# A dense feed-forward in three high/low fp32r passes, with seven ring slots for the dense stages

## What is computed

```python
def swiglu(h, w_gate, w_up, w_down):
    return (jax.nn.silu(h @ w_gate) * (h @ w_up)) @ w_down

hn = rmsnorm(h, norm_ffn[0])
h = h + swiglu(hn, ffn_w_gate[0], ffn_w_up[0], ffn_w_down[0])   # 1024 -> 3584 -> 1024
```

## Time and profile before

| | |
|---|---|
| median of 3 executions | 1668.14 us |
| the profiled execution | 1667.81 us, of which its span is 1666.0 us |
| TensorE, matmuls | 1572.7 us busy (94% of the span) |
| TensorE, weight loads | 1383.5 us (83%) |
| VectorE | 1033.7 us (62%) |
| ScalarE | 813.3 us (49%) |
| DMA | 425.16 MB, mean 255 GB/s |

### The profile page before, as it was taken

The page is one execution under the profiler, slowest core; times in us unless marked ns, Lnnn a source line. Parts: engine busy times, 40 slices in busy tenths (PEclk is TensorE's granted clock), DMA queues, the critical chain, the costliest instruction groups (busy, mean ns, idle before and its releaser), DMA issues.

```text
span 1666.0 us, 23792 instructions
## 1 busy us (share of the span) xinstructions
PE 1572.7 (94%) x9865; PEld 1383.5 (83%) x9865; DVE 1033.7 (62%) x1120; ACT 813.3 (49%) x865; POOL 0.2 (0%) x4
## 2 busy tenths in 40 slices
PE   5998999999877879999999999999999999999995
PEld 4887888888655669998998988899898898898893
DVE  5531000000144348988888888888888888888883
ACT  2511000000123227767676766767667767767662
POOL 0000000000000000000000000000000000000000
PEclk8999999999987879999999999999999999999997
DMA  9043444448211218999999999999999999999920
GB/s 347 31 149 104 152 152 151 154 153 327 99 51 51 73 55 332 357 345 352 356 342 352 357 342 350 358 344 347 358 343 347 361 347 344 363 341 344 367 83 26
DMA packets 62050, 425.16 MB, mean 255 GB/s; under 512 B 7805, under 2 KB 10106, under 8 KB 10746
## 3 DMA queue, kind: packets, MB, share of 16 engines
q1 hardware_dynamic: 60240, 422.60, 68.4%
q10 hardware_dynamic: 1706, 1.06, 0.2%
HBM read 422.59 MB, written 1.05 MB: 254 GB/s over the span
## 4 chain that ended last, share of the span: by engine, by line
PE 90%; DVE 4%; ACT 3%; issue 2%; ACTq 0%; DMA 0%; DVEq 0%
PE ps L1282 35%; PE ps L1004 21%; PE ps L1304 19%; PE ps L1086 6%; PE ps L1252 2%; PE ps L1270 2%; PE ps L1289 1%; DVE w_lo L886 1%; ACT w_hi L534 1%; PE ps L995 1%; DVE hn L698 1%; DVE scratch L772 1%; PE ps L1126 0%; DVE xg_mem L696 0%; PE ps L1215 0%
## 5 line engine op out<-in xcount | busy, mean ns | idle before, releaser
L886 DVE TENSOR_TENSOR w_lo<-ring,w_hi 128x2048 fp32r<-128x2048 f32 x336 | 766.4, 2290 | 126.1 <-ACT w_hi L534 120.3
L534 ACT CAST w_hi<-ring 128x2048 fp32r<-128x2048 f32 x336 | 640.0, 1910 | 263.5 <-PE ps L1282 212.1
L1004 PE MATMUL ps<-hn,ring 128*128 128x256 f32 x1312 | 304.1, 394 | 17.7 <-issue 9.0
L1004 PEld LDWEIGHTS ps<-hn,ring 128*128 128x128 f32 x1312 | 260.3, 199 | 59.3 <-issue 16.7
L1282 PE MATMUL ps<-w_hi,xg_hi 128*96 128x256 f32 x1792 | 246.6, 280 | 2.5 <-ACT w_hi L534 2.5
L1282 PE MATMUL ps<-w_lo,xg_hi 128*96 128x256 f32 x1792 | 242.2, 277 | 1.6 <-DVE w_lo L886 1.6
L1282 PE MATMUL ps<-w_hi,xg_lo 128*96 128x256 f32 x1792 | 241.7, 277 | 0.0
L1282 PEld LDWEIGHTS ps<-w_hi,xg_hi 128*96 128x96 f32 x1792 | 221.4, 162 | 16.0 <-DVE xg_lo L892 2.6
L1282 PEld LDWEIGHTS ps<-w_lo,xg_hi 128*96 128x96 f32 x1792 | 215.1, 161 | 3.2 <-DVE w_lo L886 3.2
L1282 PEld LDWEIGHTS ps<-w_hi,xg_lo 128*96 128x96 f32 x1792 | 216.0, 162 | 0.0
L743 DVE TENSOR_TENSOR work<-ps,work 128x256 f32<-128x256 f32 x28 | 11.9, 425 | 267.8 <-ACT work L475 267.8
(11 more groups left out here) (220 smaller groups left out, 931.9 us busy)
## 6 DMA issues: line engine op xcount, KB each, us to landing
ring<-in_moe_w_gate SPq DMA_DIRECT2D x112, 1024.0 KB, 5.5
ring<-in_moe_w_up SPq DMA_DIRECT2D x112, 1024.0 KB, 5.8
ring<-in_moe_w_down SPq DMA_DIRECT2D x112, 1024.0 KB, 5.7
ring<-in_ffn_w_gate SPq DMA_DIRECT2D x14, 1024.0 KB, 4.9
ring<-in_ffn_w_up SPq DMA_DIRECT2D x14, 1024.0 KB, 4.9
ring<-in_ffn_w_down SPq DMA_DIRECT2D x14, 1024.0 KB, 4.9
ring<-in_lru_w_in SPq DMA_DIRECT2D x8, 1024.0 KB, 10.2
ring<-in_attn_w_qkv SPq DMA_DIRECT2D x6, 1024.0 KB, 11.7
```

Source lines behind the costliest of these rows:

```text
L534: nc.scalar.copy(w_hi[:, n % PARTS], ring[:, s]).then_inc(hi_done, 1)
L886: V.tensor_tensor(w_lo[:, n % PARTS], ring[:, ORDER_MOE[n % SLOTS]], w_hi[:, n % PARTS].bitcast(F32), ALU.subtract).then_inc(lo_done, 1)
L1004: mm = nc.tensor.matmul(ps[:, bank, c0:c0 + T], w[:, k, col:col + P], rhs[:, k], start=(k == 0), stop=(k == KC - 1))
```

## The change

The dense feed-forward is computed as the experts are. ScalarE casts each of the 42 weight pieces to float32r (`split_ffn`), VectorE makes the low part, hn is split once into `u_hi` and `u_lo` ahead of the products, each chunk's product of silu and up into `f_hi` and `f_lo`, and TensorE makes three passes over each piece, of 16 matmuls each; the weights stay stationary. The loop over two passes of 7 chunks is written out as one sequence of 14. The banks of the down products are opened at the first down piece, and their closing matmuls are gone: the last products close them, and `f_acc` tells of the first three in the last pass.

Since `w_hi` and `w_lo` are now in use from the dense stage on, the scratch of the other stages moves into ring slots 7 to 10, and the split activations overlay slots 11 to 13. All dense stages, the recurrent block and attention load into slots 0 to 6 in turn. The experts' first seven loads use the same seven slots, the others wait for the router's first matmul. The splits of the experts are counted on from the 42 of the dense stage.

```diff
-LRU_LOADS, ATT_LOADS = 13, 10
-ORDER_FFN = [13, 0, 1, 2, 3, 4, 5]
-ORDER_ATT = [6, 7, 8, 9, 10, 11, 12, 13, 0, 1]
-ORDER_MOE = [2, 3, 4, 5] + ORDER_ATT
+LRU_LOADS, FFN_LOADS, ATT_LOADS = 13, PIECES, 10
+FIRST_FFN = LRU_LOADS
+FIRST_ATT = FIRST_FFN + FFN_LOADS
+DENSE_LOADS = FIRST_ATT + ATT_LOADS
+SPLITS = FFN_LOADS
+ORDER_MOE = [(DENSE_LOADS + n) % DENSE for n in range(DENSE)] + list(range(DENSE, SLOTS))
...
-        scr = scratch[:, :]
+        scr = ring[:, DENSE:DENSE + 4, :].rearrange("p s n -> p (s n)")
...
-        slot_of = list(range(LRU_LOADS)) + 6 * ORDER_FFN + ORDER_ATT
+        slot_of = [k % DENSE for k in range(DENSE_LOADS)]
...
+            def load_dense(k, kind, w, c0):
+                s, last = slot_of[k], k - DENSE
+                if FIRST_FFN <= last < FIRST_ATT:
+                    sp.wait_ge(lo_done, last - FIRST_FFN + 1)
+                elif last >= FIRST_ATT:
+                    sp.wait_ge(used, last - FFN_LOADS + 1)
+                elif last >= 0:
+                    sp.wait_ge(used, last + 1)
...
-                    sp.wait_ge(lo_done, PIECES * i + (n + 1))
-                    if n < SLOTS:
-
-                        sp.wait_ge(used, FIRST_MOE - SLOTS + 1 + n)
+                    if first and n < SLOTS:
+                        sp.wait_ge(used, LRU_LOADS + min(ATT_LOADS, ATT_LOADS - DENSE + n + 1))
+                    else:
+                        sp.wait_ge(lo_done, PIECES * i + (SPLITS - SLOTS + n + 1))
...
+            def split_ffn(j):
+
+                act.wait_ge(loaded[slot_of[FIRST_FFN + j]], arrive[FIRST_FFN + j])
+                if j >= PARTS:
+                    act.wait_ge(parts_used, j - PARTS + 1)
+                nc.scalar.copy(w_hi[:, j % PARTS], ring[:, slot_of[FIRST_FFN + j]]).then_inc(hi_done, 1)
+
+            for j in range(PARTS):
+                split_ffn(j)
             squares(1)
             root(1, 7)
-
-
-            for t in range(2):
-                for c in range(HALF):
+            for c in range(KC):
+                act.wait_ge(hn_ready, KC + c + 1)
+                nc.scalar.copy(u_hi[:, c], hn[:, c]).then_inc(u_hi_ready, 1)
+
+
+            for j in range(PARTS, FFN_LOADS + 1):
+                if j < FFN_LOADS:
+                    split_ffn(j)
+                what, c = FFN_PIECES[j - PARTS] if j < FFN_LOADS else ("up", NCH - 1)
+                if what == "up":
                     for f in range(2):
-                        act.wait_ge(f_gu, 2 * HALF * t + (2 * c + f + 1))
+                        act.wait_ge(parts_used, FFN_AT["up", c] + 1)
                         nc.scalar.activation(ffn_h[:, c % 2, f], ps[:, 2 * (c % 2) + f, 0:T], ACT.Silu).then_inc(f_silu, 1)
+                    for f in range(2):
+                        act.wait_ge(f_h, 2 * c + f + 1)
+                        nc.scalar.copy(f_hi[:, c % 2, f], ffn_h[:, c % 2, f]).then_inc(f_hi_ready, 1)
...
+            for j in range(PARTS):
+                split_ffn(j)
             for c in range(KC):
                 dve.wait_ge(o_proj, c + 1)
                 V.tensor_tensor(h[:, c], ps[:, c % 4, 0:T], h[:, c], ALU.add).then_inc(h_ready, 1)
             dve.wait_ge(h_ready, 2 * KC)
             normed(1, "ffn0")
-
-            for t in range(2):
-                for c in range(HALF):
+            for c in range(KC):
+                dve.wait_ge(u_hi_ready, c + 1)
+                V.tensor_tensor(u_lo[:, c], hn[:, c], u_hi[:, c].bitcast(F32), ALU.subtract).then_inc(u_ready, 1)
...
+            def ffn_gate_up(what, c):
+                j, m = FFN_AT[what, c], int(what == "up")
+                w = [a.rearrange("p (k c) -> p k c", k=KC) for a in ffn_parts(j)]
+                us = (u_hi, u_lo)
+                for a, b in PASSES:
+                    if b:
+                        pe.wait_ge(lo_done, j + 1)
                     for f in range(2):
-                        pe.wait_ge(f_h, 2 * HALF * t + (2 * c + f + 1))
-                        for d in range(KC):
-                            mm = nc.tensor.matmul(ps[:, 4 + d // 2, (d % 2) * T:(d % 2 + 1) * T], as_rows(s)[:, f, d * P:(d + 1) * P],
-                                                  ffn_h[:, c % 2, f], start=False, stop=False, skip_group_check=True)
-                            if f == 0 and d == 0 and c < HALF - 1:
+                        for k in range(KC):
+                            if j == 0 and f == 0 and b == 0:
+                                pe.wait_ge(u_ready if a else u_hi_ready, k + 1)
+                            mm = nc.tensor.matmul(ps[:, 2 * (c % 2) + f, m * T:(m + 1) * T], w[b][:, k, f * P:(f + 1) * P], us[a][:, k],
+                                                  start=(k == 0 and (a, b) == (0, 0)), stop=(k == KC - 1 and b == 1))
+                            if j == 0 and (a, b, f, k) == (0, 0, 0, 0):
                                 mm.then_inc(used, 1)
-                    mm.then_inc(used, 1)
...
+            for what, c in FFN_PIECES:
+                if what == "down":
+                    if c == 0:
+                        pe.wait_ge(rms_ready, 2)
+                        pe.wait_ge(zero_ready, 1)
+                        for b in range(4, 8):
+                            nc.tensor.matmul(ps[:, b, :], zero[:, 0:P], zero[:, :], start=True, stop=True)
+                    ffn_down(c)
+                else:
+                    if what == "gate" and c >= 2:
+                        pe.wait_ge(f_h, 2 * c - 2)
+                    ffn_gate_up(what, c)
```

More of the change, by code:

```diff
@@ L131, in sem @@
             return ctx.enter_context(nc.semaphore(name))
+        with (nc.sbuf_tensor("below", [P, 11 * SLOT], F32), nc.sbuf_tensor("u_hi", [P, KC, T], F32R) as u_hi,
+              nc.sbuf_tensor("u_lo", [P, KC, T], F32R) as u_lo, nc.sbuf_tensor("f_hi", [P, 2, 2, T], F32R) as f_hi,
+              nc.sbuf_tensor("f_lo", [P, 2, 2, T], F32R) as f_lo):
+            pass
         ring = sb("ring", [P, SLOTS, SLOT])
@@ L296, in pieces @@
             return seq
-        FFN_PIECES = pieces(HALF, 1)
+        FFN_PIECES = pieces(NCH, 1)
         FFN_AT = {piece: j for j, piece in enumerate(FFN_PIECES)}
@@ L337, in _ @@
             for k, (kind, w, c0) in enumerate(early):
[L338 to L352, removed]
+                load_dense(k, kind, w, c0)
+            ffn_w = {"gate": ffn_w_gate[0], "up": ffn_w_up[0], "down": ffn_w_down[0]}
+            for j, (what, c) in enumerate(FFN_PIECES):
+                load_dense(FIRST_FFN + j, "r" if what == "down" else "c", ffn_w[what], c if what == "down" else CHF * c)
             late = [(w_qkv, D), (w_qkv, D + CHF)] + [(w_qkv, CHF * t) for t in range(4)]
@@ L378, in _ @@
             NEXT_BODY = [(what, c, 1) for what, c, _ in BODY]
-            load(0, 0, 0, LEAD + BODY)
+            load(0, 0, 0, LEAD + BODY, first=True)
             with sp.Fori(0, E - 1) as i:
@@ L635, in _ @@
                 V.memset(xpad[:, b, 0:3], 0.0).then_inc(zero_ready, 1)
-            V.memset(small[:, 160:161], 0.0).then_inc(lo_done, SLOTS)
             V.memset(small[:, 96:160], 0.0).then_inc(zero_ready, 1)
@@ L731, in _, with split_ffn @@
                 V.tensor_tensor(yy[:, t], rr[:, t], yy[:, t], ALU.mult).then_inc(z_ready, 1)
+            def split_ffn(j):
+                dve.wait_ge(hi_done, j + 1)
+                V.tensor_tensor(w_lo[:, j % PARTS], ring[:, slot_of[FIRST_FFN + j]], w_hi[:, j % PARTS].bitcast(F32),
+                                ALU.subtract).then_inc(lo_done, 1)
+            for j in range(PARTS):
+                split_ffn(j)
             for c in range(KC):
@@ L883, in split @@
             def split(i, n):
-                dve.wait_ge(hi_done, PIECES * i + (n + 1))
-                V.tensor_tensor(w_lo[:, n % PARTS], ring[:, ORDER_MOE[n % SLOTS]], w_hi[:, n % PARTS].bitcast(F32),
+                part = (SPLITS + n) % PARTS
+                dve.wait_ge(hi_done, PIECES * i + (SPLITS + n + 1))
+                V.tensor_tensor(w_lo[:, part], ring[:, ORDER_MOE[n % SLOTS]], w_hi[:, part].bitcast(F32),
                                 ALU.subtract).then_inc(lo_done, 1)
@@ L1105, in _, with ffn_parts @@
-            for b in range(4, 8):
-                nc.tensor.matmul(ps[:, b, :], zero[:, 0:P], zero[:, :], start=False, stop=True, skip_group_check=True).then_inc(f_acc, 1)
+            PASSES = ((0, 0), (1, 0), (0, 1))
+            def ffn_parts(j):
+                pe.wait_ge(hi_done, j + 1)
+                return w_hi[:, j % PARTS], w_lo[:, j % PARTS]
+            def ffn_gate_up(what, c):
[5 more added lines that the diff above has]
+                        pe.wait_ge(lo_done, j + 1)
+                    for f in range(2):
+                        for k in range(KC):
[4 more added lines that the diff above has]
+                            if j == 0 and (a, b, f, k) == (0, 0, 0, 0):
+                                mm.then_inc(used, 1)
+                mm.then_inc(parts_used, 1)
@@ new lines, in ffn_down @@
+            def ffn_down(c):
+                j = FFN_AT["down", c]
```

(15 more changed lines are left out.)

91 lines of the change are left out of this document (34 added, 57 removed).

## The result

The changed kernel takes 1616.4 us (median of four executions, 1613.92 to 1620.1), the kernel before 1668.25 us beside it: a ratio of 0.9692 with a 95% interval of 0.9671 to 0.9713. It is 3.1% faster. The profiled execution took 1615.43 us, its span is 1613.3 us; the forecast was 1613.0, on the profiled execution of before.

A forecast was written before the change was run, and what follows sets the result against it. TensorE's unbroken dense-stage matmuls were taken as the bound. Stage -59.6, end -1.3, wait +4.1 and clock +2.0 summed to -54.8 us, from 1667.8 to 1613.0 us; range 1600 to 1634.

The forecast's parts named there:

- Three passes hide their weight loads: Dense stage: 128-column weight loads overlap the 256-element streams in all 2016 fp32r matmuls, as the experts' 96-column loads do.
- first rival: Dense stage: 128-column loads don't quite hide, 119 to 130 ns a matmul, kernel at 1623 to 1645 us; chance 12%.
- the second (225 ns): Rival for the dense stage: weight load fully exposed, 225 ns a matmul, kernel at 1836 us; chance 4%.
- 114.3 ns a matmul: Dense stage: pace taken from the experts' passes, giving 5.49 us a piece and 230.4 us for 42 pieces.
- First piece +1.6: Dense stage's start: waiting for casts, half clock and low parts makes the first piece 1.6 us longer than a steady one.
- opening +0.9: Dense stage: four bank-opening matmuls ahead of the first down piece, no longer inside a wait, add 0.9 us.
- end -1.3: Dense stage's end: closing matmuls go and additions into h start in the last pass, saving 1.3 us.
- The added wait, +4.1: After o_proj: weight splits ahead of residual additions delay the first sum of squares, TensorE idles, 4.1 us added.
- Half clock behind that wait, +2.0: After TensorE's idle behind o_proj: a stretch at half clock costs 0 to 3.4 us, taken as 2.0.
- ScalarE and VectorE hidden: Dense stage: per chunk ScalarE's 7.3 us and VectorE's 8.6 us fit beside TensorE's 16.5 us.
- Loads hidden: Dense and experts' stages: weight loads arrive before they are needed, experts' late ones by over 10 us; cost nil.
- Attention keeps its time: Attention stage: its work and time stay unchanged, except half-clock stretches falling otherwise, one worth up to 3.4 us.

The follow-up runs named there:

- e3: The changed kernel with dense-stage matmuls loading 96 weight columns instead of 128, a quarter of the output rows left out: 1613.36 us (one execution).
- e2: The changed kernel with the first three weight splits put between the residual additions and squares instead of ahead of them: 1612.37 us, ratio 0.9666.
- e11: The changed kernel with five 512-wide bf16 matmuls of zeros ahead of the last down piece: 1611.44 us, ratio 0.9661.
- e1: The changed kernel with the four bank-opening matmuls put back ahead of the first gate piece: 1609.61 us, ratio 0.9646.
- e4: The changed kernel with only the first of three passes in the dense stage, low parts still made: 1484.3 us (one execution).
- e7: e1 with one further 512-wide bf16 matmul of zeros ahead of the down piece of chunk 7: 1600.4 us, ratio 0.9601.
- e9: The changed kernel with the splits interleaved as in e2 and no bank-opening matmuls, first down products starting the accumulation: 1595.35 us, ratio 0.9565.
- e10: e9 with the experts' f32 scatter and gather matmuls ahead of the down piece instead of behind it: 1593.25 us, ratio 0.9591.
- e12: e9 with eight 512-wide bf16 matmuls of zeros ahead of the last down piece: 1611.4 us, ratio 0.9673.
- e8: e9 with four 512-wide fp32r matmuls, result unused, after the first gate piece: 1603.96 us, ratio 0.9616.

## Why the prediction was right, and where its terms were off

The time fell in the range, 3.4 us over the forecast, and the mechanism was the one forecast. That it is as near as this is in part luck: the pace cost 6.4 us more than forecast, and two terms that depend on the execution gave 3.6 back. Step by step:

- **Three passes hide their weight loads.** Right. 2016 single records, unbroken, and e3 prices the 32 more columns at 1.1 ns. The first rival (119 ns or more) and the second (225 ns) did not come. The rule on row groups, which the Trainium skill states in "TensorE: Matmul & The Clock Gate", Part 3, taken by itself, is contradicted by this trace too: a load of 128 columns, 128 rows high, goes unseen beside a stream of 256 at 113.3 ns. I read it too narrowly: the same Part, under "The mechanism", also lets a load go ahead of running matmuls where it targets the background weight buffer. With that the trace would agree; no run here shows which buffer a load goes to.
- **114.3 ns a matmul.** The term that was mis-sized. I took the mean of 113.5 ns (256 wide) and 115.8 (512 wide) from one pair of stretches, and left the other stretches' 117 ns to the bounds and the first rival, as if it were noise. They are two modes. The stage had some 160 matmuls at 113.3 and 1820 at 117.8: +6.4 us. 2016 times 1.0 ns less than my 114.3 and 2016 times 3.5 ns more is -2.0 and +7.1 us: the working should have given about 1611 and 1620 us, with a chance for each.
- **First piece +1.6, opening +0.9, end -1.3.** Measured 1.5 (144.96 less 137.96 less 5.49), 0.96 and -1.4.
- **The added wait, +4.1.** Right in place, cause and size: 3.8 us, ended by VectorE's addition, and in e2 gone but for 0.7.
- **Half clock behind that wait, +2.0.** It did not come in this execution; the tiles behind the gap take 3.45 us each. In e11's profile, after a gap of 3.71 us, one tile took 5.14: 1.7 us, beside 3.4 us at the half clock; e3's has 3.4 us of it at the same place. The gap is 3.5 to 3.6 us in e1, e4 and e7, where it did not come. So the bound was right and the value a matter of the execution.
- **ScalarE and VectorE hidden.** Right; e4 shows at what pace they would not be.
- **Loads hidden.** Right: the only wait for a dense load is that of the third cast, inside the added wait; the late loads of the experts cost nothing (1064.0 us in both, from the router's first matmul to the end).
- **Attention keeps its time.** Right for this kernel and by luck: 161.2 and 160.9. I had allowed one half-clock stretch, 3.4 us. e7, e9 and e10 show that the same stage can take 153, so the allowance was too small by half.

The misses, +6.4 for the pace, -2.0 for the clock, -1.6 for the earlier o_proj and -0.7 in the small ones, leave 2.1 us between the forecast -54.8 and the measured -52.7.

## What to carry to other kernels

Where rows of one and the same instruction form show two paces, don't average them: ask which one the new stream will be in, and forecast both. A matmul stream should not be broken by odd instructions that can stand elsewhere or go: four of 0.96 us in all came with a slower pace for 1820 others here, and without them (e9) all five executions kept to one group. And work that an engine does ahead of time belongs between the small operations that others wait for, not in front of them.

## What the runs showed of the hardware that I had not expected

- An fp32r stream of 256 elements a matmul runs in one of two paces, 113.3 ns or 117.8 ns (128 weight columns; with 96, 116.7 at the slower), both at full granted clock and without idle, with the same work of VectorE and ScalarE beside it. In the dense stage it keeps the pace for as long as like matmuls follow each other. Four to eight bf16 matmuls of zeros were followed by the other pace in four cases (113.3 to 117.8 in the changed kernel, e2 and e12, 117.8 to 113.3 in e11) and by the same in two (the openings of e3 and e11), one alone by the same (e7). What picks the pace at the start stays open: it differs between executions whose instructions are the same so far (e1 and e7, the changed kernel and e11, e9 and e8), and 512-wide fp32r matmuls did not choose it (e8).
- In the experts' stage the choice is nearly regular. By the median distance of two starts in a stretch of 48, all 26 gate/up stretches behind f32 matmuls run at 117 ns in the kernel before (at most two of 26 do not in the other profiles with its order), and 82 of 86 behind 512-wide fp32r ones at 113; with those nearly always in between (e10), 105 of 109 do.
- Attention, where TensorE has short gaps, took 159.5 to 161.4 us in eight profiles and 152.9 to 153.3 in five, with the same instructions. From its first matmul to the router's, 27 us are at 1.2 GHz in the second kind and 44 to 49 us in the first. The clock falls from 2.4 to 1.2 GHz while TensorE is idle ahead of attention; attention's first matmul came 1.4 to 1.9 us after that in the five, and 2.1 to 4.5 us in the eight. e12 moved it out of the first range by useless work and got the long attention; e11 was in the first range, but for the most part not by its useless work, and got the short one. So the relation is seen in 13 profiles; what produces it was not isolated.
